# A two-block model in fp32r on one core: the state-space stage regrouped, its second input product in plain fp32, the lag products spread among the driven ones, and three pieces of VectorE's program in other places

## What is computed

```
def s5_mixer(h, w_in, a_re, a_im, log_dt, b_re, b_im, c_re, c_im, d_skip, w_glu):
    u = (h @ w_in).reshape(bsz, seq, 64, 16)            # 64 groups of 16 channels
    ...                                                 # ab = exp(a*dt), bb = f*b, complex, 64 states
    bu_re = jnp.einsum('blgh,gph->blgp', u, bb_re)      # and bu_im
    s_re, s_im = scan of s[t] = ab * s[t-1] + bu[t]
    y = einsum(s_re, c_re) - einsum(s_im, c_im) + d_skip * u
    y = jax.nn.gelu(y.reshape(bsz, seq, 1024))
    z = y @ w_glu
    return z[..., :1024] * jax.nn.sigmoid(z[..., 1024:])
```

## Time and profile before

| | us |
|---|---|
| median of 3 runs (2174.03 to 2175.61) | 2175.26 |
| the profiled execution's own time | 2176.32 |
| its span | 2174.5 |
| busy: PE, DVE, ACT, POOL | 2083.6, 1441.0, 1082.2, 161.0 |

### The profile page before, as it was taken

One profiled execution on the slowest core, in us unless ns is written; L12 is line 12 of the kernel. 1 busy time (PEld: TensorE's weight loads), 2 busy tenths in 40 slices (PEclk: granted clock), 3 DMA queues, 4 the chain that ended last, 5 costly groups with the idle time before them and its releaser, 6 DMA issues.

```text
span 2174.5 us, 34810 instructions
## 1 busy us (share of the span) xinstructions
PE 2083.6 (96%) x15108; PEld 1808.8 (83%) x15108; DVE 1441.0 (66%) x1656; ACT 1082.2 (50%) x1269; POOL 161.0 (7%) x119
## 2 busy tenths in 40 slices
PE   6789999999999999999999999999999999999998
PEld 5778887988888888898778888888889977788886
DVE  8865774557775665685757666576558576667654
ACT  5664653574653553455553355335434564434542
POOL 1000000000000100340000020020005300002000
PEclk9799999999999999999999999999999999999999
DMA  7235555524555665564411466556546533135653
GB/s 180 40 121 155 181 190 171 175 97 152 180 193 168 218 194 175 179 209 136 136 41 60 159 210 208 180 174 203 187 155 216 190 117 116 42 116 177 197 180 124
DMA packets 259487, 342.49 MB, mean 157 GB/s; under 512 B 23335, under 2 KB 169421, under 8 KB 259335
## 3 DMA queue, kind: packets, MB, share of 16 engines
q1 hardware_dynamic: 253968, 329.95, 47.4%
q0 software_dynamic: 2768, 9.08, 1.3%
q10 hardware_dynamic: 2599, 1.23, 0.5%
HBM read 338.14 MB, written 2.10 MB: 156 GB/s over the span
## 4 chain that ended last, share of the span: by engine, by line
PE 85%; DVE 7%; ACT 3%; DMA 2%; issue 2%; ACTq 0%; POOL 0%; DVEq 0%; SPq 0%; POOLq 0%
PE acc L1926 11%; PE acc L1928 11%; PE acc L1927 11%; PE trp L2105 10%; PE acc L2105 8%; PE trp L2106 5%; PE acc L2106 4%; PE acc L1942 3%; PE trp L1926 2%; DVE w_lo L1220 2%; PE trp L1927 2%; PE trp L1928 2%; PE acc L1991 2%; PE acc L1949 1%; PE acc L2455 1%
## 5 line engine op out<-in xcount | busy, mean ns | idle before, releaser
L1220 DVE TENSOR_TENSOR w_lo<-raw,w_hi 128x2048 fp32r<-128x2048 f32 (+1 forms) x316 | 725.5, 2298 | 419.2 <-ACT w_hi L740 417.4
L740 ACT ACTIVATE w_hi<-raw 128x2048 fp32r<-128x2048 f32 (+1 forms) x316 | 594.0, 1880 | 548.9 <-PE acc L1928 211.0
L2105 PE MATMUL trp<-xT,w_hi 128*128 128x512 f32 x960 | 339.6, 397 | 0.3 <-DVE w_lo L1220 0.3
L2105 PE MATMUL acc<-xT,w_hi 128*128 128x512 f32 x768 | 271.3, 397 | 0.0
L2106 PE MATMUL trp<-xT,w_lo 128*128 128x256 f32 x960 | 269.4, 281 | 0.0
L2105 PEld LDWEIGHTS trp<-xT,w_hi 128*128 128x128 f32 x960 | 180.3, 188 | 44.4 <-DVE w_lo L1220 0.6
L2106 PE MATMUL acc<-xT,w_lo 128*128 128x256 f32 x768 | 215.5, 281 | 0.0
L1926 PE MATMUL acc<-xT,w_hi 128*128 128x256 f32 x736 | 208.9, 284 | 3.6 <-DVE w_lo L1220 3.6
L1928 PE MATMUL acc<-w_hi,hT_lo 128*128 128x512 f32 x528 | 209.3, 396 | 0.0
L1926 PE MATMUL acc<-w_hi,hT_hi 128*128 128x512 f32 x528 | 209.3, 396 | 0.0
L1927 PE MATMUL acc<-w_lo,hT_hi 128*128 128x512 f32 x528 | 209.3, 396 | 0.0
(11 more groups left out here) (414 smaller groups left out, 3449.1 us busy)
## 6 DMA issues: line engine op xcount, KB each, us to landing
raw<-in_ffn_w SPq DMA_DIRECT2D x184, 512.0 KB
raw<-in_w_in SPq DMA_DIRECT2D x60, 1024.0 KB
raw<-in_ffn_w_up SPq DMA_DIRECT2D x88, 512.0 KB
raw<-in_ffn_w SPq DMA_DIRECT2D x40, 1024.0 KB
raw<-in_ffn_w_down SPq DMA_DIRECT2D x20, 1024.0 KB
raw<-in_ssm_w_glu SPq DMA_DIRECT2D x16, 512.0 KB
raw<-in_kv_w SPq DMA_DIRECT2D x8, 1024.0 KB
raw<-in_w_branch_a SPq DMA_DIRECT2D x8, 1024.0 KB
```

The lines of the kernel that those rows point to most:

```text
L740: A(w_hi[:, p % SPL, 0:kt, :], raw[:, p % RAW, 0:kt, :], ACT.Copy).then_inc(hi_ready, 1)
L1220: V_.tensor_tensor(w_lo[:, p % SPL, 0:kt, :], raw[:, p % RAW, 0:kt, :], w_hi[:, p % SPL, 0:kt, :].bitcast(F32), ALU.subtract).then_inc(lo_ ...
L2105: mm(tile, w_hi[:, p % SPL, k, c], xT[:, k0 + k], start=i == k == 0, stop=False, skip_group_check=True)
```

## The change

1. **Start.** x comes by two transfers; DVE makes its statistics and norm before the parameter chain; ACT splits only panels 0 and 1 here and writes, next to the hi half of the turned x, its full fp32 form `xf` (a new buffer that shares memory with later ones); DVE makes the lo half from `xf` (`input_rests`).
2. **`ssm_in1` in plain fp32**: 32 products `raw` x `xf` in place of 96. Panels 2 and 3 are not split; the counters are raised by 2.
3. **Transposes of c**: the second goes to a turn bank with a semaphore of its own.
4. **Lag products spread**: `response` is gone; in `driven` each wide product is followed by the four lag products of its pair and r.
5. **CA has a buffer of its own** (it shares memory with `xT`), in four quarters; SP's wait for `CAm_ready` is gone.
6. **ACT and DVE in the stage**: clears and `cam` stand between the rounds of `within`; panels 4 and 5 are split by ACT behind `cam(3)`, panel 6 behind the GELUs; GELU has two buffers; DVE splits panel 4 behind E and 5 and 6 behind the rests of y.
7. **GLU**: the last columns are made by token halves (PE finishes token tile 0 first), with sigmoid, gating, sum, statistics and norm each by half.
8. **Scores**: on DVE `scores(4)` to `scores(7)` ahead of `softplus(0)`, `softplus(1)` and a split.
9. **Attended rests**: on DVE `low_part(0)` ahead of the four `decayed`.

```diff
@@ SP @@
-            sp.dma_start(x[:, :, :], T["x"][0].rearrange("(t p) d -> p t d", p=P)).then_inc(sem("x_in"), 16)
+            for t in range(TT):
+                sp.dma_start(x[:, t, :], T["x"][0, t * P:t * P + P, :]).then_inc(sem(f"x_in{t}"), 16)
...
-                if p == SPL + 4:
-                    sp.wait_ge(sem("CAm_ready"), 16)
@@ ACT @@
+                for k in range(2 * g, 2 * g + 2):
+                    A(xT_hi[:, k, :], trp[g][:, k % 2 * SEQ:(k % 2 + 1) * SEQ], ACT.Copy, scale=gain[:, k:k + 1]).then_inc(sem("xhi_ready"), 1)
+                for k in range(2 * g, 2 * g + 2):
+                    A(xf[:, k, :], trp[g][:, k % 2 * SEQ:(k % 2 + 1) * SEQ], ACT.Copy, scale=gain[:, k:k + 1]).then_inc(sem("xfull_ready"), 1)
+                if g == 1:
+                    split_hi(1)
...
-            split_hi(0)
-            tsplit("mix0", *gain_of("mix0"))
-            for p in range(1, SPL):
-                split_hi(p)
+            act.wait_ge(hi_ready, 2)
+            act.sem_inc(hi_ready, 2)
...
-            for f in range(RING):
-                cam(f)
+            cam(0)
+            cam(1)
+            within(3)
+            cam(2)
+            cam(3)
+            split_hi(4)
+            split_hi(5)
...
+                if j == 3:
+                    act.wait_ge(sem("first_tokens"), residuals["glu"] + 1)
+                    A(hbuf[:, 1, 0], A2(u)[:, 0, PN // 2:PN], ACT.Sigmoid).then_inc(sem("glu_gate"), 1)
+                    wait_filled(act, u)
+                    A(hbuf[:, 1, 1], A2(u)[:, 1, PN // 2:PN], ACT.Sigmoid).then_inc(sem("glu_gate"), 1)
+                    return
@@ DVE @@
+                    V_.tensor_tensor(xT_lo[:, ks, :], xf[:, ks, :], xT_hi[:, ks, :].bitcast(F32), ALU.subtract).then_inc(sem("xlo_ready"), 2)
...
+            for i in range(4, 8):
+                scores(i)
             softplus(0)
             softplus(1)
             split_lo(gemms["v0"][0][0] + SPL)
-            for i in range(4, 8):
-                scores(i)
...
+                low_part(0)
                 for t in range(TT):
                     for half in range(2):
                         decayed(t, half)
-                low_part(0)
@@ PE @@
-            features("ssm_in1", 0, use["ssm_in1"], xs)
+            out = A4(use["ssm_in1"])
+            claim(use["ssm_in1"])
+            pe.wait_ge(sem("xfull_ready"), KT)
+            for p in gemms["ssm_in1"][0]:
+                pe.wait_ge(raw_loaded[p % RAW], 32 * (p // RAW + 1))
+                _, _, k0, kt, _ = panels[p]
+                for n in range(4):
+                    for k in range(kt):
+                        ins = mm(out[:, n], raw[:, p % RAW, k, n * P:n * P + P], xf[:, k0 + k, :], start=k0 + k == 0 and n % 2 == 0,
+                                 stop=k0 + k == KT - 1, skip_group_check=True)
+                ins.then_inc(panel_used, 1)
...
                 for k in range(4):
+                    rows, pair = slice(32 * k, 32 * k + 32), 4 * f + k
                     for r in range(2):
-                        ins = mm(o[:, k, r], BT[:, f % RING, k, r, :], u_lags[:, 4 * f + k, :], start=k == r == 0, stop=True, skip_group_check=True)
-                ins.then_inc(sem("bu_filled"), 1)
-
-            def response(f):
-
-                o = trp[0][:, :].rearrange("p (f l h) -> p f l h", f=8, l=Q)
-                for lag in range(Q):
-                    for r in range(2):
-                        for k in range(4):
-                            rows, pair = slice(32 * k, 32 * k + 32), 4 * f + k
-                            mm(o[rows, f, lag, :], Bm[:, r, pair, lag, :], CT[:, r, pair, :], start=lag == f == r == 0, stop=r == 1, skip_group_check=True)
+                        ins = mm(o[:, k, r], BT[:, f % RING, k, r, :], u_lags[:, pair, :], start=k == r == 0, stop=True, skip_group_check=True)
+                        if k == 3 and r == 1:
+                            ins.then_inc(sem("bu_filled"), 1)
+                        for lag in range(Q):
+                            mm(lags_out[rows, f, lag, :], Bm[:, r, pair, lag, :], CT[:, r, pair, :], start=lag == f == r == 0, stop=r == 1, skip_group_check=True)
...
-                response(2 * g)
-                response(2 * g + 1)
+                if g == 0:
+                    pe.wait_ge(sem("CT_ready"), 1)
                 driven(2 * g)
                 driven(2 * g + 1)
```

More of the change, by code:

```diff
@@ L810, in _ @@
             act.sem_inc(sem("par_ready"), 1)
-            act.wait_ge(sem("mag_in"), 1)
-            A(par[:, 5, :], par[:, 3, :], ACT.Exp).then_inc(sem("trig_ready"), 1)
+            split_hi(0)
             u = use["cols"]
@@ L823, in _ @@
             wait_evacuated(act, u)
+            gain, _ = gain_of("mix0")
+            for g in range(4):
+                act.wait_ge(sem("turned"), 4 * tsplits["mix0"] + g + 1)
+                for k in range(2 * g, 2 * g + 2):
[4 more added lines that the diff above has]
+                    split_hi(1)
+            act.wait_ge(sem("mag_in"), 1)
+            A(par[:, 5, :], par[:, 3, :], ACT.Exp).then_inc(sem("trig_ready"), 1)
             act.wait_ge(sem("angle_ready"), 1)
@@ L891, in _ @@
                 turned_inputs(f)
-            split_hi(6)
-            for f in range(8):
+            for f in range(4):
+                token_lags(1, range(f, f + 1))
                 driven(f)
[L895 to L899, removed]
+                if f % 2:
                     turned_inputs(f + 3)
                     turned_inputs(f + 4)
+            for f in range(4, 8):
+                driven(f)
             act.wait_ge(sem("K_ready"), 4)
@@ L906, in _, with within @@
             act.wait_ge(sem("lags_ready"), 1)
-            for h in range(4):
+            def within(h):
                 if h:
@@ L1390, in _, with input_rests @@
             V_.memset(Bm[ST:P, :, :, :, 0:GH].rearrange("p r k l h -> p (r k l) h"), 0.0).then_inc(sem("Bm_cleared"), 1)
+            for t in range(TT):
+                dve.wait_ge(sem(f"x_in{t}"), 16)
+                statistics(0, t, t + 1)
+                statistics(1, t, t + 1)
+                moments(t, EPS, False)
+            norm("mix0")
+            split_lo(0)
+            def input_rests(groups):
+                for g in groups:
+                    ks = slice(2 * g, 2 * g + 2)
+                    dve.wait_ge(sem("xhi_ready"), 2 * g + 2)
+                    dve.wait_ge(sem("xfull_ready"), 2 * g + 2)
+                    V_.tensor_tensor(xT_lo[:, ks, :], xf[:, ks, :], xT_hi[:, ks, :].bitcast(F32), ALU.subtract).then_inc(sem("xlo_ready"), 2)
+            input_rests(range(2))
             dve.wait_ge(sem("par_ready"), 1)
@@ L1403, in _ @@
             step(V_.reciprocal(pr(9), pr(9)))
-            dve.wait_ge(sem("x_in"), 16)
-            statistics(0)
-            statistics(1)
-            for t in range(TT):
-                moments(t, EPS, False)
-            norm("mix0")
+            split_lo(1)
+            input_rests(range(2, 4))
             def negated(q0, q1):
```

112 lines of the change are left out of this document (66 added, 46 removed).

## The result

| | us |
|---|---|
| before, median of 4 runs (2168.16 to 2175.61) | 2174.65 |
| changed, median of 4 runs (2200.77 to 2203.54) | 2202.9 |
| ratio | 1.0135, interval 1.0114 to 1.0156 |
| profiled execution: span before, span changed | 2174.5, 2201.7 |

The changed kernel is 28 us slower, where 18 were forecast; it lies inside the range, 8 us under its upper end. The forecast of 2193 stood on the right case; the cost of the clock, PE's waits ahead of the GLU product and the GLU product itself were put too small.

The account below looks back on a forecast made before the run. TensorE, busy 96% of the span, was taken as the bound. Start, spread and stage gave +28.7 us, GLU tail −1.1, scores −3.5, attended rests −6.2: +17.9, so 2193 us, range 2158 to 2211.

Parts of the forecast that it names:

- the right case: Whole kernel: the spread order drains PE and its clock falls; 2193 us, chance 0.48.
- The spread and its price: State-space stage: each group of one wide and four lag products costs 0.72 us at full clock, 64 groups 46 us.
- narrow to narrow on one tile: Within a group: successive narrow instructions on the same column tile, taken at 34 ns each, seven 0.24 us.
- The clock: Driven stage: TensorE's clock falls soon after 51.2, a slow group costs 1.11 us, K ready at 123.0.
- About 18 groups at full clock: Driven stage: about 18 groups take 13.0 us at full clock, the other 46 take 51.1 at 1.11.
- The rival in which the clock holds: Driven stage: groups leave only drains, no idle rows, so full clock stays; 2172 us (2166 to 2178), chance 0.22.
- From K to the GLU product: End of the state-space stage: 43.1 us before becomes 40.3, so the GLU product starts at 163.3, +28.7.
- GLU: GLU tail by token halves: gating and norm of one half beside PE's last products, −1.1 us.
- That SP no longer waits for the CA copies lets panels come earlier; they are not last here: Ahead of the GLU product: weight panels load earlier and do not bound it; no time was given for this.
- Scores: Attention: the gap of 3.57 us before the products goes, with some slow clock behind it; −3.5 us.
- Attended rests: Both mixer layers: PE's 2.62 us gap goes and half the slow clock behind it; −3.1 each, −6.2 us.
- The rival in which the spread is nearly free: Driven stage: a group costs no more than 0.55 us, kernel faster, 2150 to 2165 us, chance 0.2.

Follow-up runs that it names:

- e2: The changed kernel with the four lag products behind each wide one taken on four column tiles in turn instead of one tile; 2183.41 us.
- e11: e7 with the loads of panels 4 and 5 held on SP until all driven inputs are copied; 2156.34 us.
- e1: The changed kernel with lag products back in rows of 128 over four column tiles ahead of the driven products; 2162.92 us.
- e6: e1 with panels 4, 5 and 6 split early again, among the driven products' copies and ahead of the advances; 2164.13 us.
- e7: e1 with the lag products of each block of 32 behind that block's eight driven products; 2160.39 us, again 2162.44.
- e9: e1 with low_part(0) back behind the four decayed in both layers; 2166.14 us.
- e4: The kernel before with only low_part(0) moved ahead of the four decayed, both layers; 2172.53 us, ratio 0.9991.
- e3: The kernel before with only the lag products spread behind the driven ones, as in the change; 2217.87 us.
- e12: e7 with VectorE's scores and low_part(0) back in their old places; 2164.29 us, ratio 0.9952.

## Why the prediction was right, and where its terms were off

**The spread and its price.** Right. Three of the four prices of a group were put together from single rows of the kernel before: wide first to narrow first 0.16 + 0.21 = 0.37, and 51.60 − 51.23 = 0.37 is measured. The fourth, narrow to narrow on one tile, was in no row; 34 ns was chosen between 8.5 and 61 by an argument (one round of four tiles), and e2 shows it right within about 1 ns. No run shows that the round of tiles is the reason, so that the sum, 0.72, came out to the hundredth is in part luck. The rule of the Trainium skill in "TensorEngine Tiling (Array Packing)", Key Properties, that a change of tiling mode drains the engine, is borne out by e2's rows: from the first narrow start to the next wide one are 52.12 − 51.94 = 0.18, of which the seven gaps over four tiles need 0.06; and from the wide start to the narrow one 0.37, of which a dense row of wide products would need 0.24.

**The clock.** Right in kind; its cost was put too small. Forecast: 18 groups at full clock and 46 at 1.11. Measured: full clock in 50.6 to 54.1 and 71.2 to 74.6 only, which is 5 groups each, and 54 at 1.16. That is 10 × 0.72 + 54 × 1.16 = 69.8 instead of 64.1, and it gives the 4.9 us by which Dsel is late, within 1. At full clock throughout the 64 groups would be 46.1, so the clock costs 24 us in this stage, nearly as much as the order itself (46.1 against 20.3). The term that failed is "About 18 groups at full clock", a number for which the prediction gives no working: one return of 3.4 us behind the turned inputs came, with 5 groups, and the first 3.5 us had 5. The price of a slow group was near: 1.11 taken, 1.16 measured. The rival in which the clock holds fell. The rule behind it, in the Trainium skill's "TensorE: Matmul & The Clock Gate", Why this matters for your kernels, speaks of idle gaps; here the records show no idle gap in 77 us, and the clock was at 1.2 GHz for 70 of them.

**From K to the GLU product.** 40.3 forecast, 170.04 − 127.9 = 42.1 measured. ACT's account was right: behind the four rounds its eight copies and two splits end at 160.91, 33.0 after K, where the forecast has 24.8 + 5.2 + 3.8 = 33.8. From there to the product are 9.1 us, and 134.58 − 127.92 = 6.7 before, which the forecast kept. In them PE has two of its three idles of 1.52, 1.79 and 2.33 among the 512 small products (L2281), put down to "issue", as it had 1.48 and 0.65 before. They come 127 products, 254 instructions, apart, and each ends 2.2 to 2.7 us behind the start of an instruction packet (e11). The term that was left out is this wait. The changed kernel's timeline of PE:

```profile
156.30 3.11 PE L2281 MATMUL acc<-Bm,CAm 128*32 128x64 f32 x197
160.93 1.99 PE L2281 MATMUL acc<-Bm,CAm 128*32 128x64 f32 x127 [1.52 <-issue]
164.71 1.99 PE L2281 MATMUL acc<-Bm,CAm 128*32 128x64 f32 x127 [1.79 <-issue]
169.02 1.09 PE L2281 MATMUL acc<-Bm,CAm 128*32 128x64 f32 x61 [2.33 <-issue]
```

**GLU.** −1.1 forecast, +1.8 measured. The tail did shrink: from the end of the product to the FFN 9.08 before (178.27 to 187.35, the latter in the earlier trace rows) and 8.41 now (216.17 to 224.58). But the product itself went from 43.69 to 46.13. The sentence that failed is "That SP no longer waits for the CA copies lets panels come earlier; they are not last here": they are last in e1, and in the changed kernel a slow start of the product hides it. `raw` holds two panels, and with their splits moved behind the CA copies no slot comes free before 165, 5 us ahead of the product. ACT and SP of the changed kernel:

```profile
179.58 1.92 ACT L743 ACTIVATE w_hi<-raw 128x2048 fp32r<-128x2048 f32 x1 [6.21 <-DMA raw<-in_ssm_w_glu]
...
191.49 1.92 ACT L743 ACTIVATE w_hi<-raw 128x2048 fp32r<-128x2048 f32 x1 [6.21 <-DMA raw<-in_ssm_w_glu]
...
200.78 1.92 ACT L743 ACTIVATE w_hi<-raw 128x2048 fp32r<-128x2048 f32 x1 [4.55 <-DMA raw<-in_ssm_w_glu]
```

```profile
165.25 0.37 SPq L628 DMA_DIRECT2D raw<-in_ssm_w_glu  x1
165.66 0.65 SPq L629 DMA_DIRECT2D raw<-in_ssm_w_glu  x1
174.46 0.37 SPq L628 DMA_DIRECT2D raw<-in_ssm_w_glu  x1
```

PE itself waits little for them here. Its longest stop in the changed kernel's product is the first line, and the window below it covers the first 3.7 us, nearly all at the lower clock, behind the idle of 2.33:

```profile
205.17 0.47 PE L1979 MATMUL acc<-w_hi,xT 128*128 128x512 f32 x1 [0.57 <-DVE w_lo L1252]
```

```profile
170.04:173.74 3.70, 3.70 (x13) 2.92 (x10) 2.20 (x2) 3.08 (x3) 0.00 (x0) 0.54 0.08 26
```

The products up to 174.49 take 4.45 us, and the same ones 2.89 before: the slow start costs 1.6. In e1 it is the other way round, with full clock at the start and a longer wait:

```profile
160.73 0.47 PE L1979 MATMUL acc<-w_hi,xT 128*128 128x512 f32 x1 [1.88 <-DVE w_lo L1252]
```

So the +2.4 of the changed kernel is 1.6 of clock and 0.6 of panels; and since e1 is as long (45.83) without the slow clock, the late panels would have held the product at about this length anyhow. e6 undid the late splits and also started at full clock; there the product took 43.66. The two causes are told apart by these profiles, not by an edit of one alone.

**Scores.** −3.5 forecast, −1.3 measured (+37.8 to +36.5; e1, e2 and e7 the same). The 3.57 went, and "next late is the split for the v product, about 2 us" was right in place and in size, 1.90. What failed is "with it some slow clock behind it": in this profile the slow clock came behind the new idle instead. In e6 and e9, with the same idle (1.88 and 1.90) and full clock behind it, the stretch gains 3.0 and 2.9.

```profile
490.37 0.50 PE L1979 MATMUL acc<-w_hi,xT 128*128 128x512 f32 x1 [1.90 <-DVE w_lo L1252]
...
491.22 0.63 PE L1979 MATMUL acc<-w_hi,xT 128*128 128x512 f32 x1
491.64 0.63 PE L1980 MATMUL acc<-w_lo,xT 128*128 128x512 f32 x1
```

These are the products behind the new idle, 0.63 each where at full clock they are 0.39.

**Attended rests.** −6.2 forecast. The gap went, and this profile shows −4.0 and −3.7 in the two mixers, more than forecast. By the medians it is less: e4 gives 0.9991 for both layers together, an interval that takes in 1, and e9 no difference; e3 has −1.3 in the second mixer without the move. What failed is that the place was priced and nothing but the Y copies was let give back what it gained; e4's slow stretch at the solve does.

**Sum.** In the profiled executions: +35.5 to the GLU product, +2.3 to the norm ahead of attention, −1.3 over attention, −4.0 and −3.7 in the two mixers, −1.8 between them (e3, without the moves there, shows −1.8 in the stretch from 1237 to 1428 too, and e1, with them, 0.1, so it is hardly the work of the change), makes +27.0, and the span shows +27.2. At the first product of the FFN the forecast has +27.6 and the profile 224.58 − 187.35 = +37.2: all of the miss of 9.3 us stands there already. By the medians the two moves on VectorE gain 3.5 us (e12 against e7, with intervals that overlap), where 9.7 were forecast. The rival in which the spread is nearly free fell with the first row of groups.

## What to carry to other kernels

Before small products are put between large ones, count how often the tile shape changes and how many of the small ones in a row use the same tile. The price of a change can be read from a handful of rows; that of the same tile needs a row that has it. A PE that the profile calls busy can still be half asleep: look at the granted clock of the stretch, too. Of a step that moves a split or a copy later, ask which ring slot it frees, and who loads into that. Where the profile says "issue" in a long row of small products, look for a packet of the instruction queue ahead of PE's restart. And a gap closed ahead of a stage with loose, small products can come back in it through the clock.

## What the runs showed that was not expected

- Four narrow fp32 products (eight instructions, 128x32 tile, 16 columns) on one column tile take 0.35 us from first start to the next wide one; over four tiles 0.18.
- PE stands still by 2.2 to 4.4 us inside rows of narrow lag products, at a point where nothing in its program waits (every kernel here with the products in rows), and not in the slower, spread order; each such idle ends 2.2 to 2.7 us behind the start of a 16 KB packet of PE's instructions.
- A kernel that beats both: e11, e1's order by block with panels 4 and 5 held, 2156.34 us, ratio to before 0.9915 (0.9898 to 0.9932). e7, without the hold, is not told from it.
